# Deferring each row's eviction, convolution and SiLU behind the heads' step in the second mixing

## The reference, cut to what matters

```
proj = h @ w_in                            # the 57 rows, 1024 -> 128 columns each
qkv = silu(causal_depthwise_conv(qkv, w_conv))
q = l2norm(q) * DK ** -0.5; k = l2norm(k)
A = where(strict, (k*beta) @ k.T * L, 0)   # for each head and chunk; L = exp(decay_i - decay_j)
T = inverse(A + I)                         # built by doubling, five levels
w = T @ (k*beta*exp(decay)); u = T @ (v*beta)
```

## Time and profile before

| what | us |
|---|---|
| median of three runs | 3462.91 (3462.8 to 3464.23) |
| profiled execution, its own time | 3464.78 |
| its span | 3463.0 |
| mean granted TensorE clock | 0.967 of full |
| PE busy | 3294.6 (95% of the span) |
| DVE busy | 2049.1 (59%) |
| ACT busy | 1328.1 (38%) |
| rows and heads stage (2087 to 2676) | 589 |

### The profile page before, as it was taken

How to read it: one execution, slowest core, us unless ns; L and a number is a source line. 1 busy time by engine, 2 the same in 40 slices (tenths; PEclk the granted TensorE clock), 3 DMA queues, 4 the chain that set the end, 5 groups by cost and what they waited for, 6 DMA issues and landing times.

```text
span 3463.0 us, 41094 instructions
## 1 busy us (share of the span) xinstructions
PE 3294.6 (95%) x16321; PEld 2722.7 (79%) x16321; DVE 2049.1 (59%) x3543; ACT 1328.1 (38%) x2338; POOL 528.5 (15%) x547
## 2 busy tenths in 40 slices
PE   8999999999999999999899997899898999999998
PEld 5764889998888888888788875778686667778887
DVE  5765987776888888887555435445443345443332
ACT  3131238883444444444322224444443124232221
POOL 0001009971222222221000000000000000000000
PEclk9999999999999999999899998999899999999999
DMA  6426234569999999996355422121121122222222
GB/s 253 138 70 221 74 123 173 191 218 345 335 329 333 338 330 327 338 327 250 105 187 183 144 70 91 58 86 67 64 83 55 41 82 79 90 79 96 96 94 75
DMA packets 190207, 574.42 MB, mean 166 GB/s; under 512 B 16576, under 2 KB 82112, under 8 KB 171712
## 3 DMA queue, kind: packets, MB, share of 16 engines
q1 hardware_dynamic: 152144, 367.96, 30.4%
q0 software_dynamic: 37872, 203.84, 16.0%
HBM read 523.89 MB, written 47.84 MB: 165 GB/s over the span
## 4 chain that ended last, share of the span: by engine, by line
PE 84%; DVE 9%; ACT 3%; POOL 2%; DMA 1%; issue 1%; SPq 0%; DVEq 0%; ACTq 0%; POOLq 0%
PE ps L231 11%; PE ps L232 10%; PE ps L233 10%; PE ps L1602 5%; PE ps L1603 5%; PE ps L1601 5%; PE ps L1362 4%; PE ps L1364 4%; PE ps L1363 4%; PE ps L240 4%; PE ps L581 2%; PE ps L316 2%; PE ps L171 1%; DVE Wl L223 1%; PE ps L584 1%; POOL peerg_OH L1354 1%
## 5 line engine op out<-in xcount | busy, mean ns | idle before, releaser
L223 DVE TENSOR_TENSOR Wl<-W,Wh 128x1024 fp32r<-128x1024 f32 x363 | 438.6, 1209 | 706.5 <-ACT Wh L217 700.3
L217 ACT ACTIVATE Wh<-W 128x1024 fp32r<-128x1024 f32 x363 | 377.6, 1041 | 567.2 <-PE ps L233 532.1
L1362 PE MATMUL ps<-peer_Hh,Wh 128*128 128x384 f32 x1024 | 349.5, 341 | 8.9 <-DVE Wl L223 8.9
L1364 PE MATMUL ps<-peer_Hh,Wl 128*128 128x384 f32 x1024 | 346.3, 338 | 0.0
L1363 PE MATMUL ps<-peer_Hl,Wh 128*128 128x384 f32 x1024 | 346.0, 338 | 0.0
L1570 POOL DMA_INDIRECT peerv_UV<-peer_uv,peer_EX x128 | 209.8, 1639 | 641.1 <-DVE peer_Y L1638 583.5
L1601 PE MATMUL ps<-peerv_VH,peer_HTh 128*128 128x512 f32 x768 | 299.0, 389 | 2.2 <-DVE peer_HTl L1664 2.2
L1603 PE MATMUL ps<-peerv_VH,peer_HTl 128*128 128x512 f32 x768 | 300.5, 391 | 0.0
L1602 PE MATMUL ps<-peerv_VL,peer_HTh 128*128 128x512 f32 x768 | 300.3, 391 | 0.0
L231 PE MATMUL ps<-f_Hh,Wh 128*128 128x512 f32 x672 | 262.3, 390 | 2.2 <-DVE Wl L223 2.2
L233 PE MATMUL ps<-f_Hh,Wl 128*128 128x512 f32 x672 | 261.5, 389 | 0.0
(11 more groups left out here) (497 smaller groups left out, 6499.3 us busy)
## 6 DMA issues: line engine op xcount, KB each, us to landing
W<-peer_u SPq DMA_DIRECT2D x128, 512.0 KB, 8.0
peerv_VR<-peer_v SPq DMA_DIRECT2D x128, 512.0 KB
gates_dram<-peerg_GB SPq DMA_DIRECT2D x12, 2048.0 KB, 7.3
peerv_GR<-gates_dram SPq DMA_DIRECT2D x32, 768.0 KB, 8.6
f_AW<-w_ada POOLq DMA_DIRECT2D x48, 512.0 KB, 4.2
W<-w_gate SPq DMA_DIRECT2D x44, 512.0 KB, 3.2
W<-w_up SPq DMA_DIRECT2D x44, 512.0 KB, 3.2
swa_AW<-w_ada POOLq DMA_DIRECT2D x32, 512.0 KB, 4.5
```

Of the source, the lines that this page charges most:

```text
L217: A.then_inc(e.activation(w_parts(i)[0], w_raw(i), ACT.Copy), ("w_hi", i))
L223: V.then_inc(e.tensor_tensor(lo, w_raw(i), hi.bitcast(F32), SUB), ("w", i))
L1362: e.matmul(o, hi[:, k, :], H2[0][:, k, 0:TD], start=k == 0, stop=False)
L1364: ins = e.matmul(o, lo[:, k, :], H2[0][:, k, 0:TD], start=False, stop=k == 7)
```

## The change

The rows' generators on ACT and DVE get a second `yield` in the middle of each iteration. `row_steps` takes the first part of the rows' work, then the heads' step, then the second part. On ACT the first part is w_hi(n+1), the decay's exponentials at n = 1, and the norm's square root; the second is SiLU and square, or the eviction. On DVE the first part is w_lo(n+1) and the norm's work; the second is the convolution. On PE the second part is empty, so PE's order stays. The keys' generators get second yields as well; their work stays in the first part of its iteration. The words "first branch's tiles still spread over the heads" in the change's name are of a part that the diff doesn't touch.

```
--- before.py
+++ after.py
@@ -2026,6 +2026,7 @@
 
     def row_steps(rows, make_head):
 
+
         todo, live, n = list(range(8)), [], -1
         while rows or todo or live:
             if rows:
@@ -2035,6 +2036,8 @@
             if todo and at_row["qkv", todo[0], 2] < n and len(live) < NCX:
                 live.append(make_head(todo.pop(0)))
             live = [g for g in live if next(g, "end") != "end"]
+            if rows:
+                next(rows)
 
     NROW = len(ROWS)
     norm_of = {at_row["qkv", h, c]: 2 * h + 1 - c for h in range(8) for c in (1, 0)}
@@ -2061,6 +2064,7 @@
                     ins = e.matmul(ps(6 + m % 2)[:, tb:tb + 1], AN[:, m // 2, sl], ones[:, 0:1], start=True, stop=True)
                 PE.then_inc(ins, ("nsum", m))
             yield
+            yield
 
     def rows_act(e):
         for n in range(NROW + 2):
@@ -2175,15 +2191,17 @@
             PE.wait_ge(e, ("lat", "uk", n))
             A.then_inc(e.activation(KN[:, n, :], ps((NROW + n) % 2), ACT.Copy), ("lat", "uk", n))
             yield
+            yield
 
     def keys_dve(e):
-        yield
-        yield
+        for _ in range(4):
+            yield
         PE.wait_ge(e, ("nbc", 15))
         lat_norm_dve(e, "k", 2, 6)
-        yield
-        yield
+        for _ in range(4):
+            yield
         lat_scale_dve(e, "k", KL, 2, "g_kv_lat_2", 7)
+        yield
         yield
 
     def head_pe(e, h):
```

More of the change, by code:

```diff
@@ L2177, in keys_act @@
             yield
+            yield
     def keys_dve(e):
-        yield
-        yield
+        for _ in range(4):
+            yield
         PE.wait_ge(e, ("nbc", 15))
         lat_norm_dve(e, "k", 2, 6)
+        for _ in range(4):
+            yield
+        lat_scale_dve(e, "k", KL, 2, "g_kv_lat_2", 7)
         yield
-        yield
-        lat_scale_dve(e, "k", KL, 2, "g_kv_lat_2", 7)
         yield
```

## The result

The changed kernel takes 3440.4 us (median of 5 runs, 3439.7 to 3445.8); the kernel before took 3462.8 (3456.2 to 3464.2) beside it. The ratio is 0.9944, with a 95% interval of 0.993 to 0.9959: faster by 0.41 to 0.70%. The forecast was 3440. The profiled execution took 3439.8 us (span 3438.0, mean granted clock 0.971), 25.0 less than that of before.

What follows compares the result with a forecast made beforehand. PE bounds the kernel, with local losses where it waits or runs at low clock. Stalls 3.1+3.1+3.4+3.3+5.2+1.1, clock 3.8+1.0 and cost -0.7 sum to 23.3 us: forecast 3440 us, range 3432 to 3455.

Steps and rivals of the forecast that it cites:

- Stalls that go: PE's waits at head steps in iterations n of `row_steps`, mostly L171 transposes, vanish or shrink once the second part moves behind.
- n=25: Step 3 of a head, qkv row: convolution, SiLU and square leave the path; wait 5.20 falls to 1.77, gaining 3.4 us.
- n=5 and n=40: Step 2 of a head, qkv rows: only the convolution leaves the path, the norm chain stays; 3.1 + 3.1 us gained.
- n=41: Step 3 of a head, qkv row: as n=25, but a norm stays ahead; wait 5.68 falls to 2.4, gaining 3.3 us.
- n=22, 38, 54: Step 3 of a head that is alone: L2276 runs inside the row, the 1.72 waits go; 5.2 us in all.
- The step for n=3: A step 0: row 5's 2.53 us wait shrinks as convolution and Exp group overlap, less one table load; 1.1 us gained.
- Clock: Slow clock behind n=22, 38, 54 mostly goes: 3.8 us (bounds 0 and 6.7), plus 1.0 behind the shortened stalls.
- What the edit costs: Qkv iterations: the DVE-ACT loop gains two products, loses two copies, +0.25 per iteration, keeps pace; -0.7 us for all.
- The rule on table loads: Trainium skill's 2.66 us per switch, against 1.28 in the trace, would cut the gain to about 15 us, 3448.
- The loop did not become the bound: Rival, 13%: ACT's copies stay in the loop, 0.96 longer in 13 two-head qkv iterations; 12.5 us back, 3452.
- The stalls did not stay: Rival, 5%: head steps at 5, 25, 40, 41 are held by something other than the eviction; 3461.
- The clock did not fall in two-head work: Rival, 6%: small gaps ahead of the norm sum (L2061) drop the clock in 13 iterations, costing 35 us; 3475.

Runs made afterwards that it cites:

- The two halves: The runs of ACT's part alone and DVE's part alone, each against the kernel before: 3454.9 us and 3462.6 us, against 3462.9.
- ACT's part alone: Against the kernel before, only ACT's SiLU, square and evictions go behind the heads' step; DVE keeps its order: 3454.9 us against 3462.9 (0.9977).
- before's second profile: The kernel before, unchanged, run and profiled once more: 3458.9 us in one run beside 3463.4.
- DVE's part alone: Against the kernel before, only DVE's convolution goes behind the heads' step, except at n=25 and 41; ACT keeps its order: 3462.6 us against 3462.9 (0.9999).

## Why the prediction held

**Stalls that go.** All of the named stalls went or shrank as named. The two halves show which engine each needs; n=25 and 41 need both. By the row starts (starts of the rows on either side of the site):

- n=5 and n=40: 3.1 + 3.1 predicted. At n=40 3.0 (row 40 to 41, -15.25 to -18.28). At n=5 3.0 too: row 6 stands at -4.00, of which 1.0 is from n=3 (row 5 starts 0.31 later and is 1.30 shorter).
- n=25: 3.4 predicted, 3.9 measured, of which 3.4 are the wait. What was left of it is 1.77, as taken from n=9.
- n=41: 3.3 predicted with 2.4 left; 3.05 measured with 2.45 left (5.68 - 2.45 = 3.2 of wait).
- n=22, 38, 54 with the clock term of 3.8: 2.5, 3.3 and 3.2 predicted, 2.7, 4.3 and 4.3 measured. Row 24 was to start 2.5 sooner and starts 2.7 sooner. The wait for Wl ahead of it (0.61) is the limit that was named: eviction and w_hi behind the Exp group. w_hi at n=22 starts at 2313.63; 2317.5 less the 3.7 by which row 22 had moved in the profile's own time is 2313.8.

**The step for n=3 failed in its way, not in its size.** "Bounds 0 and 2.5; I take 1.1" was the term. The wait of 2.53 ahead of row 5 is gone, but 1.56 of it stands ahead of L2064, for the square now follows Exp; PE's score matmuls behind it (L2222, L2223) then took 3.1 us (2135.88 to row 5 at 2138.97) where they had taken 2.0. Row 5 started 0.31 later than before and was 1.3 us shorter (6.03 instead of 7.33): the slow stretch had moved from row 5 to the matmuls ahead of it. What is left is the difference of the two waits, 2.53 - 1.56 = 1.0, by another way than forecast. The step worked with the wait of row 5 alone and looked at no other instruction of PE that needs the square. The run of ACT's part alone shows what is hidden there: without DVE's overlap the same site costs 4.0.

**Clock.** The sum came out well partly by luck. The term of 3.8 (its parts 0.8, 1.6 and 1.5 make 3.9) rests on slow rows behind the three waits, and before's second profile had the first of them (row 23) at the full clock with the wait unchanged, 5.74 us instead of 7.38. In the run of DVE's part alone rows 39 and 55 are fast too (5.75 instead of 8.36 and 8.12), with the waits of 1.72 still ahead of them. Only the 1.7 us of a wait are earned in every execution; what the clock added, less the new wait for Wl, was 1.0 at n=22 and 2.6 each at n=38 and 54.

The whole stretch from row 0 to row 56 shows how the shares missed. PE's idle time in it fell from 53.5 to 38.0 us, and the rest, the same instructions, from 478.5 to 468.7: 15.5 us of waits and 9.8 that I put down to the clock, where the terms of the prediction were 18.5 and 4.8. The named stalls gave 18.8, but new and longer small waits took 3.3 of it (Wl 1.9, L2345 0.9, L2064 in the pairs 0.5) where 0.7 was the term. Before's second profile has 54.2 and 474.3, so against it the clock gives only 5.6. Too little for the clock and too little for the cost cancelled in the sum. Over five runs each the medians differ by 22.4 us; how much of that the clock holds in an average execution no run separates.

**What the edit costs.** The loop kept pace as reckoned. Behind n=11 (row 12 to 13) 0.49 us are lost (0.3 predicted) and in the rest of the pair none: row 13 stands at -3.98, row 22 at -3.96. DVE's timeline of after at n=14, beside the earlier trace rows, show the margin: w_lo ends at 2250.31, and row 16 starts at 2251.65, 1.3 us later, where it was 2.3. From the convolution's start to w_lo's end it is 6.6 us where it was 7.6, so ACT's two copies (0.96) did leave the loop.

```profile
2243.67 0.74 DVE L2134 TENSOR_SCALAR gdnc_KD<-ps,vecs_sb 128x512 f32<-128x512 f32 x1
2244.45 2.32 DVE L2137 SCALAR_TENSOR_TENSOR gdnc_KD<-ps,vecs_sb,gdnc_KD 128x511 f32<-128x511 f32 x3
2249.08 1.23 DVE L223 TENSOR_TENSOR Wl<-W,Wh 128x1024 fp32r<-128x1024 f32 x1 [2.31 <-ACT Wh L217]
```

The new waits for Wl and L2064 total 3.9 us, not under 3. And row 56 stands 25.4 sooner but the stage ends only 23.2 sooner (2653.4, where "near 2653" was forecast). The 2 us between them are the clock again. In the keys' steps behind row 56 the head that is alone has its wait of 1.72 in both kernels; the transposes behind it, before and then after:

```profile
2636.46 0.66 PE L171 MATMUL ps<-consts_sb,gdnh_c 128*128 128x128 f32 x4 [1.72 <-ACT gdnc_KD L2276]
...
2611.41 1.12 PE L171 MATMUL ps<-consts_sb,gdnh_c 128*128 128x128 f32 x4 [1.72 <-ACT gdnc_KD L2294]
```

and the sixteen matmuls of L2250 take 3.65 us where they took 2.36. From row 56 to the stage's end it is 57.1 and 58.2 us in before's two profiles, 59.1 and 58.1 in those of the changed kernel, so this is no cost of the edit that the runs could show. The stage's clock is 0.94, where 0.95 or more was forecast. The other 1.8 us of the span lie behind the stage, in work that the change doesn't touch.

**The rule on table loads.** The second load around n=22 takes 1.28 us (2311.85) and the eviction starts 0.01 after its end (2313.14). No drain of the size that the Trainium skill gives (ScalarE: Activation LUTs, What ACT_TABLE_LOAD costs) stands in these rows, and the gain by it (15 us; its terms, three of 2.8 and one of 1.4, in fact leave 13.5) would have been 7 or more less than was measured.

**The rivals.** The loop did not become the bound, but half of the change makes it one. The stalls did not stay: the waits fell by 3.0 at n=5 and 40, 3.4 at n=25 and 3.2 at n=41. The clock did not fall in two-head work: 1.00 in 2200 to 2300, with the new waits ahead of L2064 at 0.23 and 0.26 us in the pairs. The case against this rival was stronger than the prediction had it: the largest gap in 2200 to 2300 of the kernel before is not 0.8 but the 1.77 at 2204.76, and the clock read 1.00 all the same. The micro-idles that the Trainium skill warns of (TensorE: Matmul & The Clock Gate, A second HAM failure mode: psum-queue depth-cycling) brought no loss here: in rows 12 to 17 the granted clock is 1.00 in all twelve profiles, even in DVE's part alone, with its wait of 1.13.

**The range.** The low end of 3432 is said to take all of the clock's bounds; these give 3440 - 2.9 - 3.0 = 3434. And 117 x 0.19 is 22, not 23. Neither changes the forecast.

## What to carry to other kernels

Where an engine in order serves two streams, put the work whose inputs are long ready and for which the bound engine waits ahead of the work that waits for that engine's newest result; then look at both helper engines, since moving it on one alone can leave the wait in place or lengthen the loop between them (here 8 us and nothing for the halves, 22 for both). Cost a move by listing what joins each loop and what leaves it, and every consumer on the bound engine, not only the one that waited before. Before a slow row is credited to the stall ahead of it, look at a second profile of the same kernel.

## What the hardware showed

Two executions of the kernel before had the same L171 waits to 0.5 us a line and differed by 2.4 us in this stage, in the lengths of rows behind waits, some up and some down: row 7 8.61 or 7.34, row 23 7.38 or 5.74, row 25 6.89 or 8.21 us. Two executions of the changed kernel agreed in every row to 0.05 us.

Behind a wait of 1.72 us (n=22, 38, 54 and in the keys' steps) the granted clock over the next 8 us was anything from 0.57 to 1.00. Behind the wait of 1.77 us at n=9 it was 1.00 in all eight profiles that have this wait. Behind waits of 2.4 to 5.7 us some row nearly always ran slow (row 42 took 7.08 to 7.70 us in all four profiles of the two kernels). What decides it for the shorter waits stays open.
